# Output products by token block, behind attention and at the end of block 2, with the next product begun on the first half of the tokens

## What is computed

```
for l in range(2):                                  # the "layers" l = 0, 1
    h = rmsnorm(x, g_pre[l]) * (1 + scale) + shift
    u_val, u_gate, g_conv, c_q, c_kv, k_idx, w_idx, g_attn = split(h @ w_in[l])
    y_conv = conformer_conv(...) * silu(g_conv)     # 512 features, ends in a product with w_pw2
    y_attn = dsa_attention(...) * silu(g_attn)      # 512 features
    y = concatenate([y_conv, y_attn]) @ w_out[l]    # the output product, 1024 x 1024 x 1024
    x = x + gate * rmsnorm(y, g_post[l])
h = rms_norm(x, norm_mix)                           # "block 2"
x = x + hybrid_mixer(h) @ w_out_2                   # again 1024 x 1024 x 1024
h = rms_norm(x, norm_mlp)
x = x + square(relu(h @ w_up)) @ w_down             # the MLP, 4096 wide
out = rms_norm(x, norm_final)
```

## Time and profile before

| what | value |
|---|---|
| median of 3 runs | 3333.64 us (3332.24 to 3339.71) |
| the profiled execution | 3333.65 us |
| its span, first to last instruction | 3331.8 us |
| PE busy | 3049.6 us (92%) |
| DVE, ACT, POOL busy | 1804.0, 1091.8, 956.8 us |
| mean granted PE clock | 0.953 |

### The profile page before, as it was taken

How to read it: one execution, slowest core, us unless ns; L and a number is a source line. 1 busy time by engine, 2 the same in 40 slices (tenths; PEclk the granted TensorE clock), 3 DMA queues, 4 the chain that set the end, 5 groups by cost and what they waited for, 6 DMA issues and landing times.

```text
span 3331.8 us, 49239 instructions
## 1 busy us (share of the span) xinstructions
PE 3049.6 (92%) x20177; PEld 1927.5 (58%) x20394; DVE 1804.0 (54%) x2991; ACT 1091.8 (33%) x1912; POOL 956.8 (29%) x958
## 2 busy tenths in 40 slices
PE   7989988998779969997999999999998899999997
PEld 7449773885439646873555655654656644444443
DVE  2584892666489973767365265365353333333334
ACT  2352651664356634654122122222221310000001
POOL 2301383002203571012423322323222233333330
PEclk9997999999899989998999999999898899999998
DMA  7313231002102321003101111111102111111101
GB/s 241 126 57 118 77 137 54 30 11 102 67 13 77 115 89 49 14 28 128 51 26 38 51 38 39 38 39 51 39 13 102 39 51 51 51 51 51 51 26 57
DMA packets 49168, 207.19 MB, mean 62 GB/s; under 512 B 4488, under 2 KB 9776, under 8 KB 32304
## 3 DMA queue, kind: packets, MB, share of 16 engines
q1 hardware_dynamic: 42288, 195.63, 16.5%
q10 hardware_dynamic: 6656, 8.39, 0.8%
HBM read 187.22 MB, written 16.79 MB: 61 GB/s over the span
## 4 chain that ended last, share of the span: by engine, by line
PE 75%; DVE 15%; issue 4%; ACT 3%; DMA 1%; POOL 1%; DVEq 0%; SPq 0%; ACTq 0%; POOLq 0%
PE big L270 17%; PE big L271 17%; PE big L269 17%; PE banks L269 4%; PE banks L270 4%; PE banks L271 4%; PE banks L994 3%; DVE arena L1614 2%; PE banks L861 1%; DVE arena L1835 1%; PE big L548 1%; PE banks L548 1%; DVE arena L2004 1%; DVE arena L1817 1%; DVE arena L1949 1%
## 5 line engine op out<-in xcount | busy, mean ns | idle before, releaser
L511 POOL CAST w_hi<-stage 128x512 bf16<-128x512 f32 x432 | 284.7, 702 | 1880.5 <-PE big L271 1142.6
L518 POOL TENSOR_TENSOR w_lo<-stage,w_hi 128x512 bf16<-128x512 f32 x520 | 676.4, 1333 | 396.9 <-ACT w_hi L1129 396.2
L270 PE MATMUL big<-ht_lo,w_hi 128*128 128x512 bf16 x1381 | 526.6, 381 | 21.1 <-DVE ht_lo L1515 18.7
L271 PE MATMUL big<-ht_hi,w_lo 128*128 128x512 bf16 x1380 | 525.8, 381 | 1.4
L269 PE MATMUL big<-ht_hi,w_hi 128*128 128x512 bf16 x1359 | 517.7, 381 | 1.5
L269 PE MATMUL big<-w_hi,ht_hi 128*128 128x256 bf16 (+1 forms) x1274 | 383.8, 301 | 22.5 <-POOL w_lo L518 9.6
L271 PE MATMUL big<-w_hi,ht_lo 128*128 128x256 bf16 (+1 forms) x1276 | 384.2, 301 | 0.5 <-issue 0.2
L270 PE MATMUL big<-w_lo,ht_hi 128*128 128x256 bf16 (+1 forms) x1274 | 383.7, 301 | 0.6 <-issue 0.4
L269 PEld LDWEIGHTS big<-ht_hi,w_hi 128*128 128x128 bf16 x1408 | 140.1, 100 | 180.3 <-DVE ht_lo L1515 19.1
L271 PEld LDWEIGHTS big<-ht_hi,w_lo 128*128 128x128 bf16 x1408 | 138.4, 98 | 168.3 <-issue 3.8
L270 PEld LDWEIGHTS big<-ht_lo,w_hi 128*128 128x128 bf16 x1408 | 138.4, 98 | 162.1 <-issue 6.0
(11 more groups left out here) (319 smaller groups left out, 6095.8 us busy)
## 6 DMA issues: line engine op xcount, KB each, us to landing
stage<-in_w SPq DMA_DIRECT2D x130, 1024.0 KB, 4.8
arena<-in_w_ada SPq DMA_DIRECT2D x48, 512.0 KB, 4.2
arena<-in_x SPq DMA_DIRECT2D x16, 512.0 KB, 7.0
xs<-arena SPq DMA_DIRECT2D x16, 512.0 KB, 2.6
arena<-xs SPq DMA_DIRECT2D x16, 512.0 KB, 7.9
gt<-arena ACTq DMA_DIRECT2D x16, 256.0 KB, 2.5
arena<-gt ACTq DMA_DIRECT2D x16, 256.0 KB, 2.6
out_x<-arena SPq DMA_DIRECT2D x8, 512.0 KB, 2.6
```

Of the source, the lines that this page charges most:

```text
L270: pe.matmul(out, ah, bl, start=False, stop=False)
L271: return pe.matmul(out, al, bh, start=False, stop=stop)
L511: pool.tensor_copy(w_hi[:, n % RING, c0:c1], stage[:, n % RAW_RING, c0:c1]).then_inc(s_w_hi_split, mark(s_w_hi_split, n, q))
L518: ins = pool.tensor_tensor(w_lo[:, n % RING, c0:c1], stage[:, n % RAW_RING, c0:c1], w_hi[:, n % RING, c0:c1], ALU.subtract)
```

## The change

In both layers the whole output product moves behind attention and is made token block by token block: PSUM tile t of "big" holds all 1024 columns of 128 tokens, summed over all eight k (48 matmuls in four parts of 12). ACT squares it where it lies, and DVE reads it in place of `X_TOK`; the eight copies L1242 and the eight additions L1874 are gone. The chunk order becomes "pw2, uq, uv, oc0, oc1, oa0, oa1". In block 2 the product has the same form, and its chunks o0 to o3 are cut into quarters of 512 rows by 512 columns.

The first half of the turn is issued between the parts of token block 6. ACT and DVE work on it ahead of block 5's norm. The next product (`first_gemm`) begins with the first 512 tokens, the second half of the turn between its parts. For block 2 and the MLP the two halves are split straight from PSUM. The low part of the convolution's result moves from right behind its gate into attention's steps 3 to 6 on DVE.

```diff
-            "g2", "cv8", "cv9", "cv10", "g3", "pw2", "oc0", "oc1", "uq", "uv", "oa0", "oa1"]
+            "g2", "cv8", "cv9", "cv10", "g3", "pw2", "uq", "uv", "oc0", "oc1", "oa0", "oa1"]
@@ SP @@
-                    if n == (l + 1) * len(L_CHUNKS) + 2:
+                    if n == (l + 1) * len(L_CHUNKS) + 1:
-                if n == CHUNK_AT[(2, "o2")]:
+                if n == CHUNK_AT[(2, "up1")]:
@@ PE @@
+            def first_gemm(l, name, keys):
+                pe.wait_ge(s_w_split, when(s_w_split, CHUNK_AT[(l if l < LAYERS else 2, name)]))
+                w = chunk(l if l < LAYERS else 2, name, KT)
+                g = [take(pe, "big", *key) for key in keys]
+                def part(ct, half):
+                    for k in range(KT):
+                        if ct == 0:
+                            pe.wait_ge(s_ht_lo, when(s_ht_lo, l, half, k))
+                        ins = mm3(pe, g[ct][:, half * 512:(half + 1) * 512], [x[:, k, ct * P:(ct + 1) * P] for x in w],
+                                  [x[:, k, half * 512:(half + 1) * 512] for x in hT], k == 0, k == KT - 1)
+                part(0, 0)
+                turn_x(l, 1, (0, 1))
+                part(1, 0)
+                turn_x(l, 1, (2, 3))
+                part(0, 1)
+                part(1, 1)
+            def out_tokens(l, names, yT, first_two, ready):
+                def part(t, g, p, c, ks=range(4)):
+                    w = chunk(l, names[p][c], 4)
+                    for k in ks:
+                        ins = mm3(pe, g[:, c * 512:(c + 1) * 512], [x[:, 4 * p + k, t * P:(t + 1) * P] for x in yT],
+                                  [x[:, k, :] for x in w], p == 0 and k == 0, p == 1 and k == 3)
+                first = [take(pe, "big", "y", l, t) for t in range(2)]
+                first_two(part, first)
+                for t in range(2, NT):
+                    ready(t)
+                    g = take(pe, "big", "y", l, t)
+                    for q, (p, c) in enumerate(((0, 0), (0, 1), (1, 0), (1, 1))):
+                        if t == 6 and q < 3:
+                            turn_x(nl, 0, ((0, 1), (2,), (3,))[q])
+                        ins = part(t, g, p, c)
+                        if t == NT - 1 and q < 3:
+                            ins.then_inc(s_gemm, mark(s_gemm, "y_part", l, p, c))
+                            chunk_used(l, names[p][c], s_gemm)
@@ PE, block 2 @@
-            pe.wait_ge(s_hgrn_dve, when(s_hgrn_dve, "y2_lo", 3, 1))
-            out_proj(2, Y2)
-            transpose_x(3)
-            pe.wait_ge(s_ht_lo, when(s_ht_lo, "all", 3))
+            def first_two(part, g):
+                pe.wait_ge(s_hgrn_dve, when(s_hgrn_dve, "y2_lo", 2, 1))
+                for p, ks in ((0, range(4)), (1, range(2))):
+                    for c in range(2):
+                        pe.wait_ge(s_w_split, when(s_w_split, CHUNK_AT[(2, f"o{2 * p + c}")]))
+                        for t in range(2):
+                            part(t, g[t], p, c, ks)
+                pe.wait_ge(s_hgrn_dve, when(s_hgrn_dve, "y2_lo", 3, 1))
+                for t in range(2):
+                    for c in range(2):
+                        ins = part(t, g[t], 1, c, range(2, 4))
+                    ins.then_inc(s_gemm, mark(s_gemm, "y", 2, t))
+            out_tokens(2, (("o0", "o1"), ("o2", "o3")), Y2, first_two, lambda t: None)
+            first_gemm(3, "up0", [("up", 0, 0), ("up", 0, 1)])
@@ ACT @@
+                for i in range(NT):
+                    if i == 5:
+                        ht_half(l + 1, 0)
+                    act.wait_ge(s_gemm, when(s_gemm, "y", l, i))
+                    tok_norm(l, i, tile("big", "y", l, i)[:, :], S_SSQ, S_RSTD, "y", PB[0])
+                    act.wait_ge(s_xnew, when(s_xnew, l, i))
+                    tok_norm(l + 1, i, XB[i], S_SSQ2, S_RSTD2, "x", PB[0])
@@ DVE @@
+                    if 3 <= i < 7:
+                        gated_low(i - 3)
-                    step(dve.scalar_tensor_tensor(X_TOK[:, i, :], X_TOK[:, i, :], s_(S_RSTD + i), gate_row[:, l, :], ALU.mult, ALU.mult))
+                    step(dve.scalar_tensor_tensor(X_TOK[:, i, :], tile("big", "y", l, i)[:, :], s_(S_RSTD + i), gate_row[:, l, :], ALU.mult, ALU.mult))
+                    freed_by_step("y", l, i)
+                for i in range(NT):
+                    if i == 5:
+                        ht_half(l + 1, 0)
+                    residual(i)
```

More of the change, by code:

```diff
@@ L586, in transpose_x, with turn_x @@
                         ada_pieces(l, 1)
+            def turn_x(l, half, kps):
+                if kps[0] == 0:
+                    for j in range(4):
+                        pe.wait_ge(s_xn, when(s_xn, l, half * 4 + j))
+                for kp in kps:
+                    g = take(pe, "c2", "hx", l, half, kp)
+                    for kk in range(2):
+                        for j in range(4):
+                            k = 2 * kp + kk
+                            ins = pe.transpose(g[:, kk * 512 + j * P:kk * 512 + (j + 1) * P],
+                                               x_tok(l)[:, half * 4 + j, k * P:(k + 1) * P], ident)
+                    ins.then_inc(s_gemm, mark(s_gemm, "hx", l, half, kp))
@@ L1435, in _ @@
                             act.wait_ge(s_rs_lo, when(s_rs_lo, j - 1, n))
[L1436 removed]
+                        evac(RT[n], ACT.Relu, "up", j, n, pool="mlp" if j else "big")
                         if j >= 2:
```

275 lines of the change are left out of this document (131 added, 144 removed).

## The result

| what | before | after |
|---|---|---|
| median, timed together | 3336.68 us (3332.24 to 3339.76, 4 runs) | 3241.90 us (3239.84 to 3246.10, 4 runs) |
| span of the profiled execution | 3331.8 us | 3241.1 us |
| PE busy | 3049.6 us (92%) | 3021.7 us (93%) |
| mean granted PE clock | 0.953 | 0.967 |

The ratio is 0.972, 95% interval 0.970 to 0.974: 2.8% faster. The forecast was 3244 us, with a range of 3226 to 3274.

The account below looks back on a forecast made before the run. PE's work plus its stands, waiting for DVE or ACT to finish something for all tokens, were taken to bound the kernel. Layer 0 -27.7, layer 1 -26.4, block 2 -35.5: 3333.6 - 89.6 = 3244 us, range 3226 to 3274.

Parts of the forecast that it names:

- Head of attention: Between pw2 and attention: sooner second pw2 pair (-3.5 us) and attention start without yc tiles (-48.4) in layer 0; -2.7, -47.2 in layer 1.
- Low parts in attention: Four DVE low parts in attention's steps 3 to 6, three not hidden: +3.5 us per layer, bounds 0 and 4.9.
- So blocks 2 to 6 never wait: Output product after attention: tiles free in under 7 us, a block lasts 10.35, so PE never waits for them.
- Block 7's tile: Output product: block 5's tile is free at 14.9 us, block 7 wants it at 14.75, so +0.3 us.
- The wait before the next first product: PE waits there for block 7's L1862 and the weights' split: 4 us taken, bounds 1.5 to 8.
- Slow restart and low parts at the joint: At the next first product: 2 us for slow restart after the wait, 2 for the last low parts.
- Rival 2: Restarts do not come: short stands keep the clock at 1.00, waits at lower ends, about 12 us less, 3232; chance 0.09.
- The joint as a whole: From attention's last block's end (E) to the next first product's end: E+123.0, 20.7 us longer in layer 0, 20.0 in layer 1.
- Block 2: End of block 2: 72 matmuls start before the last low part, first "up" ends at 2632.0 instead of 2667.5, -35.5 us.
- Rival 1: Backlog on ACT and DVE, beside a slowing POOL, decides the joints: 3264 us (3258 to 3280); chance 0.18.
- Rival 3: Attention's early steps are bound by something the yc tiles covered; the turn pays, the move does not: 3269 to 3290; chance 0.05.
- Rival 4: PE's clock falls to 1.2 GHz inside all three products: +247 us, some 3490; chance 0.02.

Follow-up runs that it names:

- late low parts: Changed kernel with the convolution result's four low parts in attention's steps 40 to 43 instead of 3 to 6: 3243.8 us, ratio 0.972.
- Block 0 before block 1: Changed kernel with the attention half of the product finished for token block 0 before block 1 is touched: 3248.4 us, ratio 0.973.
- the tile taken late: Changed kernel whose next first product takes its second PSUM tile only on use, after the second turn's first half: 3240.3 us, ratio 0.971.
- the attention half alone: Changed kernel without the convolution's half of the output product in both layers, an incomplete kernel for timing only: 3180.6 us.
- the four edits together: Changed kernel with late low parts, block 0 first, late second tile with split k, and MLP tiles begun at the third: 3218.7 us, ratio 0.965.
- the filled wait: Kernel with late low parts plus 24 identity transposes in the wait before each layer's next first product: 3240.5 us, ratio 0.970.

## Why the prediction was right

The sum was -89.6 us; the profiled executions differ by 90.7, the medians by 94.8 (before against 3333.64: 91.7). By the rows, cut at the second tile of each next first product, layer 0 gave -26.4 (forecast -27.7), layer 1 -27.3 (-26.4), block 2's mixer -1.1 (nothing), block 2's end -38.8 (-35.5), and what follows lost 2.9 again (nothing). So the mechanism held in each part, but that the whole came within 1.1 us is in part luck: 3.3 us too little at block 2's end met 2.9 us that I had not counted behind it. Point by point:

- **Head of attention.** Forecast -3.5 - 48.4 = -51.9 in layer 0; L1884 starts at 536.78 where L1810 started at 588.76, -52.0. In layer 1, counted from layer 0's second tile, it is -49.8 for a forecast of -49.9. PE's idle time before the second pw2 pair is 1.36 us (forecast 1.2). The line "L1810 at about 540" under what would show it was my slip: it leaves the 3.5 us out.
- **Low parts in attention.** Forecast +3.5 with bounds 0 and 4.9, measured +5.1. This is the term that was mis-sized, as feared. Three passes of 1.22 us explain the 3.5. What I left out was the clock that fell with the short waits (0.74 over 15 us), and 0.5 us at attention's end, where DVE's two last passes are longer beside POOL. The passes cost at the gate and early in attention alike; only late in attention they cost nothing in attention's own time.
- **Start of the product.** The first row is at E+1.8, but it is the product's second matmul; the row of the first is missing from the trace. In the traces that have it, as with late low parts, it stands at E+1.46, forecast E+1.4. 7 slow matmuls are recorded behind it.
- **"So blocks 2 to 6 never wait" failed.** Block 2 waits 1.83 us in each layer. I had reckoned with a block every 10.35 us, but the first two blocks end only 2.6 us apart. And the table load before ACT's root (1.28 us) was not in my 3.2 us. Block 0 before block 1 removed the wait.
- **Block 7's tile.** Forecast +0.3, measured none: the scaling of block 5 ended at 816.9.
- **The wait before the next first product.** Forecast 4 (1.5 to 8), measured 3.25 in both layers, for L1938 as I said. The split of the weights stood right beside it: with the tile taken late, PE waited 0.59 us for that.
- **Slow restart and low parts at the joint.** Forecast 2 and 2, measured 0 and 2.4. Rival 2 was right here, though not because the wait was short: four other kernels had slow matmuls behind the same wait, or one of 2.5 us. That none came in the two profiled executions of the changed kernel is luck as far as the runs tell; they could have cost up to 3 us in each layer.
- **The joint as a whole.** Layer 0: forecast E+123.0, measured E+122.6. In layer 1 I gave 20.0 us more than before, and it was 17.2: the low parts that come straight from PSUM were never waited for, and the restart was absent.
- **Block 2.** Forecast -35.5 from the last low part on, measured -38.8. Of its three steps the head start is worth 17.8, near the 16 us wait that it removed, and the wait for block 7's addition is 1.5, as reckoned. Over-sized was the first "up": 24.4 us in place of 26.9, as none of the 1.8 for restart and low parts came and the turned tiles took 3.8 in place of 4.4. Not foreseen was the 1.21 us wait of the second "up" for its tile; it went with one line. The other 1.5 us of the 2.9 were lost behind PE's last matmul, in the final norm and the stores, where nothing was changed.

Rival 1 would have needed a wait over 8 us: the longest is 3.25. Rival 3 falls with the rows of attention's head. Rival 4 falls with clock 0.98 over the layers' products and 1.00 over block 2's. There the trace speaks against the rule of the Trainium skill that stood beside it ("TensorE: Matmul & The Clock Gate", section "A second HAM failure mode: psum-queue depth-cycling").

The contention that I weighed by the Trainium skill ("SBUF — State Buffer", section "Who interferes with whom") is in the rows. POOL's split of cq took 8.2 us, in place of the 11.0 beside a busy DVE before. These are DVE rows beside the split that follows it (POOL casts until 830.35 and subtracts until 836.69):

```profile
829.30 1.28 DVE L1938 SCALAR_TENSOR_TENSOR arena<-big,small,arena 128x1024 f32<-128x1024 f32 x1
830.62 1.93 DVE L1941 TENSOR_TENSOR arena<-arena 128x1024 f32<-128x1024 f32 x1
832.46 0.15 DVE L1526 RECIPROCAL small<-small 128x1 f32<-128x1 f32 x1
832.65 1.46 DVE L1530 TENSOR_SCALAR arena<-arena,small 128x1024 f32<-128x1024 f32 x1
```

L1938, which reads PSUM and one SBUF operand, takes 1.28 us as ever, and POOL's cast beside it 2.28, as alone. L1941 with two takes 1.93 in place of 1.23, and L1530 takes 1.46 in place of 0.75. The cleanest pair is the scaling pass wholly beside POOL's subtraction. Below, the first row is L1862 of the kernel before, with two SBUF operands: 1.99 us in place of 1.29. The others are the same pass (L1943) with one operand in PSUM, in layer 1 of the kernel with the attention half alone, and POOL's subtraction around it:

```profile
824.76 1.99 DVE L1862 SCALAR_TENSOR_TENSOR arena<-arena,small 128x1024 f32<-128x1024 f32 x1
...
1446.88 1.28 DVE L1943 SCALAR_TENSOR_TENSOR arena<-big,small,arena 128x1024 f32<-128x1024 f32 x1
...
1442.70 5.91 POOL L520 TENSOR_TENSOR w_lo<-stage,w_hi 128x512 bf16<-128x512 f32 x4
```

The trace agrees with the rule, which also names `tensor_scalar` in its fast two-port mode as one that can contend. The wait came out 0.75 us shorter than forecast; that this is why was not tried.

## What to carry to other kernels

Where PE waits for passes over all tokens, make the product by token block and begin the next one on the first half: the half turns alone were worth 41 us or more here, and the head start in block 2 another 18. Before removing a wait, look for the next one behind it and move work in front of that too: by its own rows, the second tile taken late cost 2 us alone and gained 7 with work moved in front of the next wait, and the four edits together gained 20. And judge an edit of a few microseconds by the rows of its own stretch: block 2's mixer, which no edit touched, took from 938.6 to 948.9 us in these kernels, and 942.9 and 945.5 in two executions of the same one.

## What the runs showed of the hardware

- The same wait of 3.25 to 3.28 us of PE was followed by no slow matmul in both layers of two kernels (one of them profiled twice), by 8 in both layers of one, by 14 in both of one. In one it was 14 and none in its first profiled execution, 14 and 13 in its second. What decides is open; it is not the length of the wait. Behind a wait of 0.58 to 0.63 us there was none in both layers of four kernels, one of which filled the wait with work that computes nothing.
- One DVE pass of 1.62 us once lasted 18.33 us, in the kernel with the filled wait. These are its row and those of POOL's splits beside it:

```profile
2549.05 18.33 DVE L1537 TENSOR_SCALAR arena<-arena,small 128x1024 f32<-128x1024 f32 x1
...
2548.97 4.52 POOL L520 TENSOR_TENSOR w_lo<-stage,w_hi 128x512 bf16<-128x512 f32 x4
...
2562.32 4.50 POOL L520 TENSOR_TENSOR w_lo<-stage,w_hi 128x512 bf16<-128x512 f32 x4
```

POOL worked without a break from 2540.05 to 2566.82, each subtraction in the 4.5 us that it takes alone, and the DVE pass ended 0.56 us behind it. In the changed kernel the same pair went the other way: the pass took 1.62 us and POOL's subtraction 5.39. So the rows look as if DVE stood until POOL stopped; no run tried it. A single profiled execution can be off by that much.
